# Encoder step with a hierarchical mixture of experts: the last expert's tokens finished apart, final loads released by the last expert but one, outputs stored by index

## What is computed

```
h = x + mix
hn = rmsnorm(h, norm_ffn)
h = h + hier_moe(hn)                  # expert(x) = (silu(x @ w_eg[e]) * (x @ w_eu[e])) @ w_ed[e]
                                      # out = gate_0 * expert_0(x) + gate_1 * expert_1(x)
y_prompt = rmsnorm(h[:, N_META:], norm_final)
y_sample = rmsnorm(h, norm_final)
```

## Time and profile before

| | |
|---|---|
| median of 3 runs | 1041.88 us (1039.87 to 1043.06) |
| profiled execution | 1040.4 us, of which span 1038.6 us |
| PE busy | 995.3 us (96%) |
| DVE busy | 564.6 us (54%) |
| ACT busy | 243.8 us (23%) |
| POOL busy | 105.2 us (10%) |
| DMA | 263.22 MB, mean 253 GB/s |
| chain that ended last | PE 78%, DMA 17%, DVE 3%, issue 1%, ACT 1% |

### The profile page before, as it was taken

One profiled execution on the slowest core, in us unless ns is written; L12 is line 12 of the kernel. 1 busy time (PEld: TensorE's weight loads), 2 busy tenths in 40 slices (PEclk: granted clock), 3 DMA queues, 4 the chain that ended last, 5 costly groups with the idle time before them and its releaser, 6 DMA issues.

```text
span 1038.6 us, 33500 instructions
## 1 busy us (share of the span) xinstructions
PE 995.3 (96%) x14706; PEld 785.9 (76%) x14706; DVE 564.6 (54%) x1285; ACT 243.8 (23%) x531; POOL 105.2 (10%) x169
## 2 busy tenths in 40 slices
PE   7999999999999999999999999999999999999976
PEld 7785858585868686847787888888887787878842
DVE  2433535353544444426866666766756657566637
ACT  2352323232232323122011111111111110111125
POOL 0110101010101010101110111111111110101000
PEclk8999999999999999999999999999999999999989
DMA  9921010100010101656999999999999999999959
GB/s 313 337 95 42 1 42 0 40 0 40 0 40 0 40 0 41 243 205 237 370 362 419 421 420 422 420 425 418 424 418 419 423 414 426 414 418 420 388 190 390
DMA packets 55329, 263.22 MB, mean 253 GB/s; under 512 B 11385, under 2 KB 12985, under 8 KB 47067
## 3 DMA queue, kind: packets, MB, share of 16 engines
q1 hardware_dynamic: 44506, 235.19, 56.2%
q0 software_dynamic: 8192, 18.06, 4.6%
q10 hardware_dynamic: 2592, 9.44, 2.3%
HBM read 247.18 MB, written 27.19 MB: 264 GB/s over the span
## 4 chain that ended last, share of the span: by engine, by line
PE 78%; DMA 17%; DVE 3%; issue 1%; ACT 1%; SPq 0%; DVEq 0%; ACTq 0%
PE bank L1504 19%; PE bank L1790 18%; DMA arena<-in_w_ed 16%; PE bank L1622 11%; PE bank L1802 8%; PE bank L1556 6%; PE bank L1809 5%; PE bank L1490 1%; PE bank L1602 1%; DMA arena<-in_w_in 1%; PE bank L1874 1%; PE bank L1563 1%; PE bank L1619 1%; PE bank L1881 1%; PE bank L1883 1%
## 5 line engine op out<-in xcount | busy, mean ns | idle before, releaser
L1504 PE MATMUL bank<-xnT,arena 128*128 128x128 f32 x1728 | 201.4, 278 | 3.8 <-DMA arena<-in_w_in 2.5
L1504 PEld LDWEIGHTS bank<-xnT,arena 128*128 128x128 f32 x1728 | 197.1, 193 | 6.3 <-DVE late L1020 3.2
L1790 PEld LDWEIGHTS bank<-hnT,arena 128*64 128x64 f32 x4096 | 157.0, 137 | 10.3 <-issue 5.6
L1790 PE MATMUL bank<-hnT,arena 128*64 128x88 f32 x4096 | 160.1, 239 | 3.2 <-issue 1.6
L1622 PE MATMUL bank<-arena,mixT 128*128 128x512 f32 x256 | 111.7, 593 | 0.0
L1802 PE MATMUL bank<-arena,osq 128*32 128x384 f32 (+1 forms) x768 | 85.7, 487 | 8.8 <-DMA arena<-in_w_ed 8.8
L1622 PEld LDWEIGHTS bank<-arena,mixT 128*128 128x128 f32 x256 | 47.9, 190 | 57.2 <-issue 57.1
L1309 DVE TENSOR_SCALAR mixT<-mixT 128x352 f32<-128x352 f32 x32 | 14.1, 440 | 136.5 <-ACT mixT L874 136.5
L1790 PE MATMUL bank<-xnT,arena 128*64 128x88 f32 x2176 | 87.3, 239 | 0.8 <-issue 0.8
L1278 DVE STREAM_TRANSPOSE hnT<-xs 32x256 f32<-32x256 f32 x192 | 83.4, 435 | 7.5 <-DMA xs<-hn_rows,idx_i 1.3
L1790 PEld LDWEIGHTS bank<-xnT,arena 128*64 128x64 f32 x2176 | 85.0, 137 | 1.4 <-issue 1.3
(11 more groups left out here) (265 smaller groups left out, 1053.6 us busy)
## 6 DMA issues: line engine op xcount, KB each, us to landing
arena<-in_w_eu SPq DMA_DIRECT2D x32, 2048.0 KB, 9.1
arena<-in_w_ed SPq DMA_DIRECT2D x31, 2048.0 KB
arena<-in_w_eg SPq DMA_DIRECT2D x17, 2048.0 KB
work<-in_w_eg SPq DMA_DIRECT2D x15, 2048.0 KB
hn_rows<-hs ACTq DMA_DIRECT2D x18, 512.0 KB, 3.5
arena<-pick_rows SPq DMA_DIRECT2D x18, 512.0 KB, 9.9
arena<-in_w_in SPq DMA_DIRECT2D x4, 2048.0 KB
arena<-in_w_out SPq DMA_DIRECT2D x2, 2048.0 KB, 12.8
```

The lines of the kernel that those rows point to most:

```text
L1504: last = mm(bank[n][:, m * P:(m + 1) * P], w[:, k, m * P:(m + 1) * P], xnT[:, k, :], start=k == 0, stop=k == KD - 1)
L1790: last = mm(out[q * SW:(q + 1) * SW, n * BLOCK:(n + 1) * BLOCK], w[:, k, m * P + q * SW:m * P + (q + 1) * SW], rowsT[b][:, k, :], start=k ...
```

## The change

After the change, the rows of the last expert (e = 31) no longer go through `y_dram`. In their place, early on, an extra scatter writes an old `ye[1]` to their rows, so that these hold finite numbers. SP's final loads then wait for the scatters of experts 0 to 30 only, and they go to blocks that expert 31 doesn't use. The tokens of expert 31 get tile buffers of their own: POOL gathers their `h` rows (from a copy of `h` in DRAM that SP writes during the mixer and the first expert), their two gates (from a DRAM copy that ACT writes) and the row of their other pick. DVE adds it all up with expert 31's result straight from PSUM (`own_rest`, `own_sum`), normalizes it (`own_normalize`), and POOL stores it by index. All other output stores move from SP to POOL and go by index too, with the rows of expert 31's tokens left out. `slots()` is cut in two and moved up to experts 28 and 29. PE's and the other engines' branches on `n_x` move between experts 30 and 31. `SUMS_BUSY` is removed.

```diff
-SUMS_BUSY = 7
+X_AFTER = 2
         def lot(n):
-            return arena[:, n * D:(n + 1) * D]
+            return blocks[(0, 4, 5, WORK, LATE)[n // 4]][:, n % 4 * D:(n % 4 + 1) * D]
 # SP
+            def keep_h(j):
+                sp.dma_start(h_dram[j * P:(j + 1) * P, :], h_all[:, j, :]).then_inc(s["rows_kept"], 16)
+            for j in range(TILES - 2):
+                sp.wait_ge(s["h_added"], j + 1)
+                keep_h(j)
             load_piece(1, 0, GATE)
+            sp.wait_ge(s["h_added"], TILES - 1)
+            keep_h(TILES - 2)
...
             load_piece(1, 0, DOWN)
+            sp.wait_ge(s["own_added"], 2)
+            keep_h(TILES - 1)
             sp.wait_ge(s["pe_u2"], 2)
             load_piece(1, 1, GATE)
...
-            sp.wait_ge(s["pe_d"], NE)
+            sp.wait_ge(s["pe_d"], NE - 1)
...
             for i in range(TILES):
                 for k, y in ((0, y1[i]), (1, y2[i])):
                     at_row = (PICKS * i + k) * P
                     sp.dma_start(y, y_dram[at_row:at_row + P, :])...
-            for i in range(TILES):
-                sp.wait_ge(s["tile_out"], outs_of(i))
-                if i == 0:
-                    sp.dma_start(y_sample, y2[i][0:SAMPLE, :]).then_inc(s["outs_stored"], 16)
-                else:
-                    sp.dma_start(y_prompt[(i - 1) * P:i * P, :], y2[i]).then_inc(s["outs_stored"], 16)
 # POOL
             scatter(0, 1, first=True)
+            nc.gpsimd.indirect_dma_start(y_dram, bass.IndirectOffsetOnAxis(ap=idx_i[0:STORE, NE - 1:NE], axis=0), ye[1], None, ...)
...
+            gather_own(row_f[0:BLOCK, :], table_dram, idx_i[0:BLOCK, NE - 1:NE], PICK_ROWS, s["own_in"])
             with pool.Fori(3, NE // 2) as t:
...
             scatter(NE // 2 - 2, 1)
-            for b in range(2):
-                scatter(NE // 2 - 1, b)
+            pool.wait_ge(s["rows_free"], NE - 1)
+            pool.wait_ge(s["own_idx_ready"], 1)
+            gather_own(own_h, h_dram, row_i[0:BLOCK, TOKEN_ROW:TOKEN_ROW + 1], TILES * P, s["own_in"])
+            pool.wait_ge(s["gates_kept"], 16)
+            gather_own(own_gates[0:BLOCK, 0:1], gates_dram, idx_i[0:BLOCK, NE - 1:NE], PICK_ROWS, s["own_in"])
+            gather_own(own_gates[0:BLOCK, 1:2], gates_dram, row_i[0:BLOCK, OTHER_PICK:OTHER_PICK + 1], PICK_ROWS, s["own_in"])
+            scatter(NE // 2 - 1, 0)
...
+            for b in range(2):
+                pool.wait_ge(ye_stored[b], 16 * (NE // 2))
+            gather_own(own_y, y_dram, row_i[0:BLOCK, OTHER_PICK:OTHER_PICK + 1], PICK_ROWS, s["other_in"])
+            for i in range(TILES):
+                pool.wait_ge(s["tile_out"], outs_of(i))
+                if i == 0:
+                    store_rows(y_sample, out_idx[0:SAMPLE, 0:1], y2[0][0:SAMPLE, :], SAMPLE)
+                else:
+                    store_rows(y_prompt, out_idx[:, i:i + 1], y2[i], SEQ)
+                if i == X_AFTER:
+                    pool.wait_ge(s["tile_out"], OWN_OUT)
+                    store_rows(y_prompt, row_i[0:BLOCK, PROMPT_ROW:PROMPT_ROW + 1], own_row, SEQ)
+                    store_rows(y_sample, row_i[0:BLOCK, SAMPLE_ROW:SAMPLE_ROW + 1], own_row, SAMPLE)
 # ACT
             expert(0, 1, True)
+            act.dma_start(gates_dram.rearrange("(n p) o -> p (n o)", p=P), gate_all[:, :, :].rearrange("p a k -> p (a k)"))...
             expert(NE // 2 - 1, 0)
-            expert(NE // 2 - 1, 1, last=True)
...          # the branch on n_x
+            expert(NE // 2 - 1, 1, last=True)      # copies only the three L883 parts
             for n, i in enumerate(PE_ORDER):
                 for k in range(PICKS):
                     A(diag[PICKS * n + k], ident, ACT.Copy, scale=gate_all[:, i, k:k + 1]).then_inc(s["diag_ready"], 1)
+            def own_rstd(): ...                    # Square, Ln, Exp of own_row, after tile 2
 # DVE
-            with dve.Fori(1, NE // 2 - 1) as t:
+            with dve.Fori(1, NE // 2 - 2) as t:
                 expert(t, 0)
                 expert(t, 1)
+            overflow()                             # L1335 to L1345
+            expert(NE // 2 - 2, 0)
+            slots()                                # the rest, and five instructions for out_idx
+            expert(NE // 2 - 2, 1)
+            dve.wait_ge(s["own_in"], 16)
+            V.tensor_copy(row_i[:, :], row_f[:, :]).then_inc(s["own_idx_ready"], 1)
             expert(NE // 2 - 1, 0)
-            slots()
-            expert(NE // 2 - 1, 1, last=True)
...          # the branch on n_x
+            def own_rest():
+                dve.wait_ge(s["own_in"], 16 * 4)
+                dve.wait_ge(s["other_in"], 16)
+                final.then(V.scalar_tensor_tensor(out=own_h, in0=own_y, scalar=own_gates[0:BLOCK, 1:2], in1=own_h, op0=ALU.mult, op1=ALU.add))
+            def own_sum():
+                dve.wait_ge(s["pe_d"], NE)
+                ...                                # two from PSUM, 88x384, and one of 88x256 after ACT's three copies
+            expert(NE // 2 - 1, 1, last=True)
+            own_rest()
+            combine(0)
+            combine(2)
+            own_sum()
             dve.wait_ge(s["g_fin_in"], 16)
-            combine(0)
             normalize(0)
-            combine(2)
             normalize(1)
             combine(4)
             normalize(2)
+            own_normalize()
             normalize(3)
 # PE
-            with pe.Fori(1, NE // 2) as t:
+            with pe.Fori(1, NE // 2 - 1) as t:
                 for b in range(2):
                     expert(t, b)
             pe.wait_ge(s["slots_ready"], 1)
             n_x = pe.value_load(steer[0:1, 0:1], min_val=0, max_val=EXTRA)
-            pe.wait_ge(s["ye_ready"], YE_STEPS * NE)
+            expert(NE // 2 - 1, 0)
             with pe.If(n_x > 0):
+                pe.wait_ge(s["ye_ready"], YE_STEPS * (NE - 1))
...                                                 # the two bodies, now in one branch
-            for _ in range(SUMS_BUSY):
-                mm(bank[3][:, :], ident, h_all[:, 1, half_row(0)], start=True, stop=True)
+            expert(NE // 2 - 1, 1)
             pe.wait_ge(s["diag_ready"], PICKS * len(PE_ORDER))
             for n, i in enumerate(PE_ORDER):
                 pe.wait_ge(y_in[i], 16 * PICKS)
+                if n == 2:
+                    pe.wait_ge(s["fin_ready"], DVE_ORDER.index(X_AFTER) + 2)
```

More of the change, by code:

```diff
@@ L394, in build @@
         fss_half = sb("fss_half", [P, len(PE_TILES)])
[L396 removed]
+        diag = [lot(2 * TILES + 1)[:, n * P:(n + 1) * P] for n in range(PICKS * len(PE_TILES))]
         def half_row(h):
@@ L876, in expert @@
                 if not first:
-                    act.wait_ge(ye_stored[b], 16 * t)
-                for half in range(1 if last else 2):
+                    act.wait_ge(ye_stored[b], 16 * (t + b))
+                for half in range(0 if last else 2):
                     A(ye[b][0:BLOCK, half * OWN:(half + 1) * OWN], bank[6 + half][0:BLOCK, 0:OWN], ACT.Copy).then_inc(s["ye_ready"], 1)
                 for (a, z), (n, c) in zip(TG_AT, REST_AT):
-                    if last and n != 6:
-                        continue
                     A(ye[b][a:z, 2 * OWN:D], bank[n][STORE:STORE + z - a, c:c + REST], ACT.Copy).then_inc(s["ye_ready"], 1)
@@ L889, in _ @@
             expert(0, 1, True)
+            with nc.allow_non_contiguous_dma("a gate of each row"):
+                act.dma_start(gates_dram.rearrange("(n p) o -> p (n o)", p=P), gate_all[:, :, :].rearrange("p a k -> p (a k)")).then_inc(s["gates_kept"], 16)
             with act.Fori(1, NE // 2 - 1) as t:
@@ L915, in _, with tile_rstd @@
                     A(diag[PICKS * n + k], ident, ACT.Copy, scale=gate_all[:, i, k:k + 1]).then_inc(s["diag_ready"], 1)
-            for i in range(TILES):
+            def tile_rstd(i):
                 if i in PE_TILES:
@@ L933, in _, with own_rstd @@
                 A(fss[0:r, i:i + 1], fss[0:r, i:i + 1], ACT.Exp, scale=-0.5).then_inc(s["frstd_ready"], 1)
+            def own_rstd():
+                act.wait_ge(s["fin_ready"], DVE_ORDER.index(X_AFTER) + 2)
+                own = fss_own[0:BLOCK, :]
+                final.then(A(own_spare, own_row, ACT.Square, scale=D ** -0.5, accum_out=own))
+                final.then(A(own, own, ACT.Ln, bias=eps[0:BLOCK, 0:1]))
+                A(own, own, ACT.Exp, scale=-0.5).then_inc(s["frstd_ready"], 1)
+            for i in range(TILES):
+                tile_rstd(i)
+                if i == X_AFTER:
+                    own_rstd()
         @block.vector
@@ L1345, in slots @@
                 st(V.tensor_reduce(slot_t[:, 0, :], is_e[:, :, :], AX.X, ALU.add))
+            def slots():
+                st = once.then
                 st(V.scalar_tensor_tensor(out=slot_f[:, :], in0=e_flat, scalar=float(BLOCK), in1=r_flat, op0=ALU.mult, op1=ALU.add))
```

119 lines of the change are left out of this document (85 added, 34 removed).

## The result

The changed kernel takes 1053.53 us (median; 1051.08 to 1057.59), the kernel before 1041.67 beside it: ratio 1.0116, 95% interval [1.0098, 1.0134]. It is 11.9 us slower, where I forecast 2.0 more and allowed 7.1. Twice more, unchanged and on other occasions, it gave 1.0119 [1.0102, 1.0136] and 1.0116 [1.0095, 1.0137].

The account below looks back on a forecast made before the run. Weight stream bounds the experts, PE close behind. Bytes 3.5, branch 4.5, clock 1.2 twice and ACT 3.7 put PE's sums at 1009.7; finish and store give span 1040.6, median 1043.9 us; 8-in-10 range 1036.7 to 1049.

Parts of the forecast that it names:

- Bounds and the prize: Experts bound by the weight stream, PE close behind; 14.4 us between expert 31's last matmul and PE's sums can be won.
- Bytes in the full stretch: Added DMA bytes during the experts: sum 4.4 us, 3.5 taken for expert 30's down, ends 1.5 and 6.
- the cost of the gates' writes: Gates to DRAM as 2304 pieces of 4 bytes: 2.2 us, priced from small reads; between zero and twice that.
- the dip of the earlier trace: At 516 to 532 us, DMA share 0.94: takes up 1.0 us of the added bytes.
- a rival for the writes: Gates' small writes at a doubled price: weight stream shifts 2.2 us more, 1046.1 us; chance 0.12.
- The branch: PE's skip over the extra blocks between experts 30 and 31: stops PE 4.5 us, ends 0.5 and 7.
- The clock, twice: Two PE pauses, at the branch and before the sums, lower the clock: 0 to 2.35 us each, 1.2 taken.
- the rival on the branch: Between experts 30 and 31: 7 us stop and full 2.35 us for both clock losses, 1048.7 us; chance 0.22.
- ACT: Between PE's end and its sums: diagonal matrices made after expert 31's copies, PE waits 3.7 us.
- DVE's cover: Experts 28 and 29: DVE's idle 4.5 and 5.6 us just cover `overflow()` 4.0 and remaining `slots()` 5.3, at no cost.
- the gather for `own_rest`: In the finish: issued about 993, landing 13.3 us later, DVE starts at 1006, changes nothing by itself; chance 0.06.
- The last store: After the last `normalize`: POOL's indirect store takes 4.0 us, plus 0.6 us behind the last landing.

Follow-up runs that it names:

- five edits: Changed kernel with gates as 128 runs, expert 31's gathers later, idle matmuls before PE's sums, no PE extra blocks, tiles 5 to 8 stored by SP: 1037.50 us, 0.9953.
- one group of runs: Kernel before plus small writes: 1.007; changed kernel with gates as 128 runs: 1.0045, without PE's extra blocks: 1.0037, with tiles 5 to 8 stored by SP: 1.0033.

## Why the prediction was wrong, point by point

**Bounds and the prize: right.** PE's sums could start 14.4 us after expert 31; now they start after 3.75. With five edits, two of which leave work out, the prize shows: 5.0 us under the kernel before. Of the 10.6 us at the sums, by the traces, 1.8 went to bytes ahead of expert 30's down, 2.7 to the short groups, 0.6 went between the sums and the last `normalize` (DVE's added one is the likely cause), and 1.6 to the last stores; the spans differ by the remaining 3.9 (1038.6 and 1034.7).

**Bytes in the full stretch: the cost of the gates' writes failed.** Expert 30's down came 9.5 us later where I took 3.5 with an end at 6; 6.3 of these were there at expert 28 and are the bytes' part. The price of the gates' writes came from a stretch of small reads that ran alone; it held for their own packets (2.2 us), but not for the others in flight, which it did not show. Alone they cost 7 us. The other new bytes cost nearly nothing: with the gates as 128 runs, expert 28's down stands at 943.4 where it was 943.3, and 1.0 to 1.6 us later in two more of the edited kernels without the early dip. So the dip of the earlier trace rows did take them up, as I had said, once the small writes were out of it. I had a rival for the writes, a doubled price of their own packets, 2.2 us more, at 0.12. It pointed the right way, but neither its mechanism nor its size was right: the packets' own price was not doubled, the transfers beside them were slowed. The Trainium skill ("DMA: Bandwidth & Descriptors", Specifications) says that transfers below 512 bytes become read-modify-writes; that 72-byte pieces, 128 in number, cost little and 2304 of 4 bytes much agrees in direction, but the page gives no price for others' packets, and runs of more sizes weren't made.

**The rest of the 9.5: not on my list.** 3.2 us are the short groups. I named POOL's gathers among what is queued, and looked only at what waits for them. The second thing the change does to PE, that expert 30 and 31 leave the loop and run as new code, I did not see at all.

**The branch: right.** 4.62 us for 4.5, and its removal gave 4.3 to 5.5 with the clock behind it.

**The clock, twice: right in kind, low in size.** The gate and up of expert 31 lost 2.3 us, of which expert 31 as a whole gave back 0.5, and the sums about 1.5, where I took 1.2 each; I had the full 2.35 as an end and chose the middle without a row for it. The second loss also fell into the sums, not ahead of them. (In the rival on the branch, the distance from +2.0 to the bound of 3.1 is 1.1 us, not 1.2.)

**ACT, DVE's cover, the moved `slots()`, the gather for `own_rest`: right.** 3.75 us for ACT. The final loads started at 1000.2, not at 993: expert 30's scatter was issued 6.0 us later than my sum has it (992.3), and its landing took 7.8 us, where it was 6.6. The gather, issued at 1000.9, landed 6.2 us after its issue, `own_rest` ran at 1007.25, and the sums of PE were later than DVE, as worked out.

**The last store: wrong, and the largest single miss.** 9.0 us from the last `normalize` where I took 4.6. SP knew of the landing 4.8 us after that `normalize`, where I took 4.0: POOL issued the store 1.2 us after it, and 3.6 us more passed. What I left out, the other 3.6 us of the miss, is that the program ends only when POOL has drained. The row for it was in the trace, 5.4 us behind the last scatter, hidden by 35 us of other work. A cost that is covered today had to be looked for on the engine to which the last instruction moves.

In sum, measured less forecast: bytes +2.8, short groups +3.2, end +4.4, the two clock terms +0.4, the branch +0.2: 11.0 us over my 1040.6 us of span. The three large errors had the same sign, and my range took in only one rival at a time.

## What to carry to other kernels

A DMA of a few kilobytes in 4-byte pieces to DRAM may cost more through what else is in flight than by its own packets: lay it out so that each partition writes one run. (To place it where the DMAs are idle is the other way; it wasn't tried.) When the last DMA moves to another engine, look up how long that engine's drain takes at the end of the block, even if it is hidden now. And when steps are taken out of a loop, what runs beside their first pass can matter: move an edit's index DMAs to where the engine in new code stands still anyway.

## What the runs showed of the hardware that I had not expected

- 2304 writes of 4 bytes (9 KB) beside transfers by index and a full weight stream: 7 us, with a DMA share of 1.09 to 1.15 at 122 to 157 GB/s over 8 us in the kernel before with them and three executions of the changed kernel; POOL's transfers took 73 and 79% of 13 us per MB, not 25%. As 128 runs of 72 bytes: 322 GB/s in the same window.
- POOL's drain after a DMA by index: 5.4 to 9.1 us from its start, 2.7 to 4.0 us beyond the moment at which SP saw the landing. SP's drain takes 0.01 us.
- While POOL issues DMAs by index, PE in code that it runs for the first time issued four to six matmuls about every 0.72 us, and ACT, past its loop as well, began expert 30's exponential after 6.59 us of idle time where it was 2.86 with the gathers moved. In the loop the same DMAs did nothing of the kind. That it is the fetch of instructions is likely from this, but only argued; and in one group of runs it did not happen, with the gathers issued beside the same new code.
